# Two-layer hybrid backbone on one core: modulation computed by rows in pieces spread over the layer, no barrier between layers, and the DeltaNet preparation begun in the projection

## The chip, the core and the metric

One core of a Trainium2 chip runs the whole program. The metric is the device time of one execution in microseconds (us), median over runs. Engines are named as in the profile: PE is TensorE's matmul stream and PEld its weight load, DVE is VectorE, ACT ScalarE, POOL GpSimd, SP SyncE (here it only issues DMAs). A name with q, such as POOLq, is that engine's instruction queue. A difference of 0.2% (about 10 us) is what a measurement of this kernel can tell from no change.

## The reference

1024 latent tokens and 128 context tokens go through two layers. Each layer computes, for x of shape tokens x 1024:

```python
m = jnp.einsum('...d,de->...e', jax.nn.silu(cond), w_mod) + b_mod   # 3 x 1024 outputs
shift, scale, gate = split_cols(m, (D_MODEL, D_MODEL, D_MODEL))
h = rms_norm(x, norm_w) * (1.0 + scale) + shift
proj = jnp.einsum('btd,de->bte', h, lp['w_in'])                     # 9008 columns
# proj feeds three mixers: gated DeltaNet, grouped-query attention, Mamba-2 SSD
merged = sigmoid(g_a) * branch_a + sigmoid(g_b) * branch_b + sigmoid(g_c) * branch_c
x = x + gate * (merged @ w_out)
```

The conditioning vector does not depend on x, so shift, scale and gate of both layers can be computed at any time before they are used. A last RMSNorm ends the program. All data are fp32.

## The kernel before, in words

x is kept transposed, as 8 blocks (`KT`) of 128 channels by 1152 tokens (`T`; 9 tiles of 128, the last is the context). Every large product keeps fp32 precision by three matmuls (high times high, high times low, low times high) on operands split into two rounded parts: `h_hi`, `h_lo` for the activations, `w_hi`, `w_lo` for the weights. A **group** is 256 output columns: 144 matmuls of 384 columns, with its weights loaded into `w_raw` by SP and split by DVE (`split_group`). The projection is 36 groups.

A layer, inside a loop over the two layers, is a row of stages with barriers between them. At a barrier each engine drains and waits for the other four. The stages that matter here:

- **Stage 0, norm and modulation.** ACT squares x, DVE sums, PE sums over channels, POOL takes the power -1/2 (`r_tok`), DVE spreads it on diagonals (`r_diag`), PE turns them into rows (`row_bc`). PE multiplies the two conditioning vectors by `w_mod`, six loads of 2 MB with three buffers; ACT copies the two result rows, PE turns them into columns (`mod`). Then DVE, ACT and DVE make wide, `h_hi` and `h_lo` for each of the 8 blocks ("the h chain"), and DVE splits the first weights. Barrier 0.
- **Stage 1, projection.** PE bound. ACT and DVE take the results out, POOL stores them (`leave` to `proj_d`). Barrier 1.
- **Stage 2, DeltaNet preparation**, 9 tiles: PE transposes and multiplies, ACT squares, DVE sums, POOL takes a power, ACT scales, DVE writes `g_out`. SP stores `g_out` whole (`gdn_tile_d`); the diagonal 32x32 blocks of it are also stored by themselves, for one direction by SP and for the other by POOL (`blocks_out`, `adiag_d`). POOL fills `g_row`, `g_col` and clears buffers at the stage's start. Barrier 2.
- **Stage 3, attention preparation**, 9 tiles with the chain DVE, POOL, DVE, ACT, PE, ACT. Loads of `u_raw` from `adiag_d` begin it. Barrier 3.
- Attention, SSD, DeltaNet scan and the branches follow; the change leaves them as they are, up to the last product (`w_out`), whose `merge_out` on DVE writes the new x. Barrier 13 ends the layer.

After the loop, x is transposed back tile by tile, squared, scaled and stored.

Of the kernel before, what the change touches and what calls it, by code (L numbers as in the profile page):

```python
# [80 lines left out]
NPH = 14  # L81
# [41 lines left out]
def backbone_kernel(nc, A, O, table, rope_table):  # L123
    with ExitStack() as ctx:
# [19 lines left out]
        adiag_d = dram("adiag_d", [2, P, SOLVE * SOLVE])  # L144
        adiag_p_d = dram("adiag_p_d", [2, 16, SOLVE * SOLVE])
# [137 lines left out]
        gin = [place(a, f"gin{n}", [P, 12, P]) for n in range(2)]  # L283
        g_row = [place(a, f"g_row{n}", [P, 2, GH * P], F32R) for n in range(2)]
        g_col = [place(a, f"g_col{n}", [P, 2, P], F32R) for n in range(2)]
        own = place(a, "own", [P, GH])
# [68 lines left out]
        a = fresh([ACTV[2] - 12288, 0, ACTV[2]])  # L355
        mod_rows = place(a, "mod_rows", [P, 3 * D_MODEL])
        a = fresh(WT)
        w_mod = [place(a, f"w_mod{n}", [P, KT, 2 * GW]) for n in range(3)]

        a = fresh(EV)  # L360
        x_tok = [place(a, f"x_tok{n}", [P, D_MODEL]) for n in range(2)]
        f_gain = place(a, "f_gain", [P, D_MODEL])
        rows_wide = place(a, "rows_wide", [P, D_MODEL])
        rows_in = place(a, "rows_in", [P, P])
# [50 lines left out]
        mod_col = sem("mod_col")  # L415
# [87 lines left out]
        ain_in = [sem(f"ain_in{i}") for i in range(2)]  # L503
        state_in = [sem(f"state_in{i}") for i in range(2)]
# [5 lines left out]
        g_pstored = [sem(f"g_pstored{i}") for i in range(2)]  # L510
# [9 lines left out]
        mod_in = [sem(f"mod_in{i}") for i in range(3)]  # L520
        scan_in = [[sem(f"scan_in{d}{i}") for i in range(2)] for d in range(2)]

        def barrier(e, l, k):

            e.sem_inc(waits_held, 1)
            e.drain().then_inc(phase_done, 1)  # L526
            e.wait_ge(phase_done, l * 5 * NPH + 5 * (k + 2))
            e.sem_inc(waits_held, 1)
# [6 lines left out]
        def first_barrier(e):  # L535
            e.drain().then_inc(phase_done, 1)
            e.wait_ge(phase_done, 5)
# [59 lines left out]
        def blocks_out(e, t, d):  # L597

            for c in range(4):
                at = slice(c * SOLVE, (c + 1) * SOLVE)  # L600
                src = g_out[t % 2][at, 6 * d].rearrange("p (h t) -> p h t", t=P)[:, :, at]
                dst = adiag_d[d, c * 32 + t * 4:c * 32 + t * 4 + 4] if t < NS else adiag_p_d[d].rearrange("(h c) n -> c h n", c=4)[c]
                e.dma_start(dst.rearrange("h (j i) -> j h i", i=SOLVE), src).then_inc((g_pstored if d else g_stored)[t % 2], 16)

        def stored_count(l, t):


            return (l * (5 - t % 2) + t // 2) * 5 * 16

        def pool_stored(l, t):  # L610

            return (l * (5 - t % 2) + t // 2) * 4 * 16
# [84 lines left out]
        def _(sp):  # L697
            sp.dma_start(cst[:], table.rearrange("p (c n) -> p c n", n=P)).then_inc(cst_in, 16)
            sp.dma_start(rope[:], rope_table.rearrange("p (t a d) -> p t a d", t=NT, a=2)).then_inc(cst_in, 16)

# [4 lines left out]
            for t in range(NT):  # L705
                if t >= 2:
                    sp.wait_ge(tok_turned, t - 1)
                src = xsm[t * P:(t + 1) * P] if t < NS else A["x_prompt"].rearrange("b t d -> (b t) d")
                sp.dma_start(x_tok[t % 2][:], src).then_inc(tok_in[t % 2], 16)
            sp.drain().then_inc(phase_done, 1)  # L710

            with sp.Fori(0, DEPTH) as l:

                wm = A["w_mod"][l].rearrange("(k p) n -> p k n", p=P)
                for g in range(6):
                    if g >= 3:
                        sp.wait_ge(mod_used, l * 6 + g - 2)
                    sp.dma_start(w_mod[g % 3][:], wm[:, :, g * 2 * GW:(g + 1) * 2 * GW]).then_inc(mod_in[g % 3], 16)
                sp.wait_ge(mod_used, l * 6 + 4)
                arrive(sp, l, 0)  # L720

# [3 lines left out]
                for run, (kind, pairs, col, _) in enumerate(PROJ_RUNS):  # L725
# [8 lines left out]
                    base += 2 * pairs  # L734
                sp.wait_ge(row_made, l * 2 + 1)
# [6 lines left out]
                sp.dma_start(flat_rows[512:576], ssm_rows[0:64, 4].bitcast(F32)).then_inc(row_out, 16)  # L742
                sp.wait_ge(row_out, l * 80 + 80)
# [3 lines left out]
                def g_store(t):  # L747
                    sp.wait_ge(gp_kk, l * NT + t + 1)
                    blocks_out(sp, t, 0)
                    sp.wait_ge(gp_v, l * NT + t + 1)  # L750
                    sp.dma_start(gdn_tile_d[t], g_out[t % 2][:]).then_inc(g_stored[t % 2], 16)
# [13 lines left out]
                for p in range(2):  # L765
                    sp.wait_ge(g_stored[p], (l + 1) * (5 - p) * 5 * 16)
                    sp.wait_ge(g_pstored[p], (l + 1) * (5 - p) * 4 * 16)


                for d in range(2):  # L770
                    sp.dma_start(u_raw[:, d], adiag_d[d]).then_inc(beta_in, 16)
                    sp.dma_start(u_raw[32 * d:32 * d + 16, 2], adiag_p_d[d]).then_inc(beta_in, 16)

                with sp.Fori(0, 3) as i:
                    for p in range(2):
                        sp.wait_ge(transposed, nth(l, i * 2, 1, 5) + (p + 1))
                        ain_load(i * 2 + (p + 2), p)
                sp.wait_ge(transposed, nth(l, 7, 1, 5))
                ain_load(8, 0)
# [153 lines left out]
                barrier(sp, l, 13)  # L933
# [3 lines left out]
            for t in range(NT):  # L937
                sp.wait_ge(x_new, t + 1)
# [7 lines left out]
        def _(pe):  # L946
# [3 lines left out]
            pe.wait_ge(cst_in, 80)  # L950
            pe.transpose(bank(7, 24), rows_in[0:24], ident[0:24, 0:24]).then_inc(cond_t, 1)
            for t in range(NT):
                pe.wait_ge(tok_in[t % 2], 16 * (t // 2) + 16)
                if t >= 2:
                    pe.wait_ge(first_c, t - 1)
                for k in range(KT):
                    last = pe.transpose(bank(2 * (t % 2), P, k * P), x_tok[t % 2][:, k * P:(k + 1) * P], ident)
                last.then_inc(tok_turned, 1)
            first_barrier(pe)
# [8 lines left out]
            with pe.Fori(0, DEPTH) as l:  # L968


                def mod_columns(first, count, dst):

                    pe.wait_ge(mod_row, l * 6 + (first + count) // 4)
                    pe.sem_inc(waits_held, 1)
                    for b in range(count):
                        last = pe.transpose(bank(dst, 2, 32 + 2 * b), mod_rows[0:2, (first + b) * P:(first + b + 1) * P], ident[0:2, 0:2])
                    last.then_inc(mod_col, 1)
                for g in range(6):
                    pe.wait_ge(mod_in[g % 3], l * 32 + 16 * (g // 3) + 16)
                    if g >= 2:  # L980
                        pe.wait_ge(mod_row, l * 6 + g - 1)
                    for k in range(KT):
                        last = pe.matmul(bank(6 + g % 2)[0:2], cond[:, k:16:8], w_mod[g % 3][:, k],
                                         start=(k == 0), stop=(k == KT - 1))
                    last.then_inc(mod_used, 1)
                    if g == 1:
                        pe.wait_ge(n_add, l * (KT - 1) + KT - 1)
                        for t in range(NT):
                            last = pe.matmul(bank(2, 1, t), tmp[:, t * P:(t + 1) * P], ones[:, 0:1], start=True, stop=True)
                        last.then_inc(n_mm, 1)  # L990
# [1563 lines left out]
```

## Time and profile before

| | us |
|---|---|
| median of 3 runs | 4798.93 (4793.77 to 4803.2) |
| profiled execution, its time | 4772.26 |
| profiled execution, span of the core | 4770.5 |

Busy share of the span: PE 86%, DVE 45%, ACT 22%, POOL 13%. The profiled execution ran 0.56% below the median of the runs.

The page's table of slices cuts the span into 40 equal parts. A timeline row gives start, duration, engine and line, operation, output and inputs, and in brackets how long the engine sat idle before it and what released it.

### The profile page before, as it was taken

To read this page: it belongs to the slowest core of one execution; us is meant where nothing else is said; L and a number is where in the kernel's file an instruction comes from. 1 tells how busy PE (TensorE), PEld (TensorE's weight loads), DVE (VectorE), ACT (ScalarE), POOL (GpSimd) and SP (SyncE) were. 2 spreads that over 40 slices of the span, in tenths; PEclk is the share of its full clock that TensorE was granted. 3 is DMA by queue.
4 is the path that set the end of the run, shared out by engine and by line. 5 is a ranking of instruction groups with operands and counts; after the bars stand their busy time and mean duration, and the time that the engine had idled before them with its cause. 6 is when DMAs were issued, how large, how long until landed. Compare 5 with 4: busy or idle time off the path is not lost.

```text
span 4770.5 us, 64010 instructions
## 1 busy us (share of the span) xinstructions
PE 4117.2 (86%) x24849; PEld 3850.1 (81%) x24849; DVE 2153.1 (45%) x2548; ACT 1038.3 (22%) x1855; POOL 600.1 (13%) x725
## 2 busy tenths in 40 slices
PE   6999999974898968868879999999649989678698
PEld 2999999974887838868849999999648877478688
DVE  3432541116665782245345235311266667723563
ACT  2110111013444510220021012010233454102200
POOL 0010000025100150000000000000350002400000
PEclk7999999987998979989989999999859989789799
DMA  6222222225002442533252222222530034435332
GB/s 225 83 90 81 80 89 94 84 93 192 13 14 77 158 159 95 159 120 115 78 182 91 87 79 85 89 93 75 172 102 14 14 100 158 141 109 164 102 123 92
DMA packets 421562, 497.62 MB, mean 104 GB/s; under 512 B 77602, under 2 KB 357508, under 8 KB 413772
## 3 DMA queue, kind: packets, MB, share of 16 engines
q1 hardware_dynamic: 354840, 384.79, 24.5%
q0 software_dynamic: 33856, 94.70, 5.3%
q10 hardware_dynamic: 32636, 15.04, 1.1%
q8 instruction: 146, 2.39, 0.2%
q14 instruction: 84, 0.69, 0.0%
HBM read 325.08 MB, written 169.37 MB: 104 GB/s over the span
## 4 chain that ended last, share of the span: by engine, by line
PE 71%; DVE 7%; DMA 6%; issue 6%; SPq 3%; DVEq 3%; POOL 2%; ACT 1%; POOLq 1%; ACTq 1%
PE PSUM L680 15%; PE PSUM L682 14%; PE PSUM L681 14%; PE PSUM L1121 5%; PE PSUM L1268 4%; PE PSUM L1142 3%; PE PSUM L1110 2%; PE PSUM L1111 2%; SPq L899 2%; PE PSUM L1371 1%; PE PSUM L1372 1%; PE PSUM L1373 1%; DMA g_XY<-xy_d 1%; PE PSUM L1227 1%; DMA xin<-proj_d 1%
## 5 line engine op out<-in xcount | busy, mean ns | idle before, releaser
L680 PE MATMUL PSUM<-h_hi,w_hi 128*128 128x384 f32 x3456 | 1160.3, 336 | 38.2 <-DVEq L526 30.0
L681 PE MATMUL PSUM<-h_lo,w_hi 128*128 128x384 f32 x3456 | 1158.6, 335 | 0.0
L682 PE MATMUL PSUM<-h_hi,w_lo 128*128 128x384 f32 x3456 | 1158.2, 335 | 0.0
L680 PEld LDWEIGHTS PSUM<-h_hi,w_hi 128*128 128x128 f32 x3456 | 652.1, 189 | 39.3 <-issue 30.2
L681 PEld LDWEIGHTS PSUM<-h_lo,w_hi 128*128 128x128 f32 x3456 | 652.2, 189 | 0.0
L682 PEld LDWEIGHTS PSUM<-h_hi,w_lo 128*128 128x128 f32 x3456 | 651.9, 189 | 0.0
L664 DVE CAST w_hi<-w_raw 128x2048 fp32r<-128x2048 f32 (+1 forms) x104 | 118.9, 1143 | 722.6 <-PE PSUM L682 584.1
L1781 POOL DMA_DIRECT2D proj_d<-leave x140 | 80.9, 578 | 1684.6 <-ACT leave L1497 650.7
L680 PE MATMUL PSUM<-b_hi,w_hi 128*128 128x384 f32 x768 | 263.7, 343 | 27.9 <-DVE w_lo L666 10.8
L1121 PE MATMUL PSUM<-v_all,prob_t 128*128 128x64 f32 x2336 | 283.6, 276 | 2.3 <-DVE prob_t L2260 2.2
L1121 PEld LDWEIGHTS PSUM<-v_all,prob_t 128*128 128x128 f32 x2336 | 279.1, 196 | 4.6 <-issue 3.5
L681 PE MATMUL PSUM<-b_lo,w_hi 128*128 128x384 f32 x768 | 261.9, 341 | 0.0
L682 PE MATMUL PSUM<-b_hi,w_lo 128*128 128x384 f32 x768 | 261.6, 341 | 0.0
L2197 DVE TENSOR_REDUCE row_max<-PSUM 128x1 f32<-128x1152 f32 (+1 forms) x144 | 178.3, 1238 | 158.1 <-PE PSUM L1111 158.0
L666 DVE TENSOR_TENSOR w_lo<-w_raw,w_hi 128x2048 fp32r<-128x2048 f32 (+1 forms) x104 | 221.3, 2128 | 8.7 <-issue 0.9
L1497 ACT ACTIVATE leave<-PSUM 128x1152 f32<-128x1152 f32 x60 | 68.1, 1135 | 678.8 <-PE PSUM L682 678.8
L1142 PE MATMUL PSUM<-cst,prob 128*128 128x128 f32 x1168 | 162.2, 283 | 14.9 <-ACT prob L1602 9.7
L680 PEld LDWEIGHTS PSUM<-b_hi,w_hi 128*128 128x128 f32 x768 | 148.6, 194 | 31.7 <-issue 25.9
L1268 PE MATMUL PSUM<-g_XY,g_t 128*128 128x128 f32 x576 | 84.2, 308 | 102.3 <-DMA g_XY<-xy_d 93.8
L1110 PE MATMUL PSUM<-k_hi,q_now 128*128 128x512 f32 (+1 forms) x400 | 152.4, 381 | 16.7 <-ACT prob_t L1608 12.7
L1602 ACT ACTIVATE prob<-PSUM,row_max 128x1152 f32<-128x1152 f32 (+1 forms) x144 | 161.4, 1121 | 21.8 <-PE PSUM L1142 11.6
L1268 PEld LDWEIGHTS PSUM<-g_XY,g_t 128*128 128x128 f32 x576 | 78.7, 219 | 105.6 <-DMA g_XY<-xy_d 52.3
(310 smaller groups left out, 6588.2 us busy)
## 6 DMA issues: line engine op xcount, KB each, us to landing
w_raw<-in_w_in SPq DMA_DIRECT2D x70, 1024.0 KB, 4.8
proj_d<-leave POOLq DMA_DIRECT2D x140, 512.0 KB, 2.9
g_t<-gdn_tile_d SPq DMA_DIRECT2D x36, 1024.0 KB, 8.2
gdn_tile_d<-g_out SPq DMA_DIRECT2D x18, 1792.0 KB, 7.6
wide<-proj_d SPq DMA_DIRECT2D x48, 576.0 KB, 3.7
w_mod<-in_w_mod SPq DMA_DIRECT2D x12, 2048.0 KB, 16.9
xs<-ssm_tok_d SPq DMA_DIRECT2D x36, 640.0 KB, 4.7
ssm_tok_d<-x_rest SPq DMA_DIRECT2D x36, 512.0 KB, 3.2
```

The source lines that it names most:

```text
L664: dve.tensor_copy(w_hi[p][:, 0:kt], w_raw[p][:, 0:kt])
L666: dve.tensor_tensor(w_lo[p][:, 0:kt], w_raw[p][:, 0:kt], w_hi[p][:, 0:kt].bitcast(F32), ALU.subtract).then_inc(w_ready[p], 1)
L680: pe.matmul(dst, wh, x_hi[:, k, lo:hi], start=(k == 0), stop=False)
L681: pe.matmul(dst, wh, x_lo[:, k, lo:hi], start=False, stop=False)
L682: last = pe.matmul(dst, wl, x_hi[:, k, lo:hi], start=False, stop=(k == kt - 1))
L899: sp.dma_start(gd[d]["XY"][t % 2][at, :, at], src.rearrange("h x (j i) -> j h x i", i=SOLVE)).then_inc(scan_in[d][t % 2], 16)
L1110: pe.matmul(dst, q_now[u][:, h], k_hi[:, g, col:col + width], start=True, stop=False)
L1121: last = pe.matmul(bank(7, AD, h * AD), prob_t[s][:, j], v_all[:, kt, g * AD:(g + 1) * AD], start=(j == 0), stop=(j == len(key_tiles) - 1))
L1142: last = pe.transpose(dst, prob[s][:, j * P:(j + 1) * P], ident)
L1268: last = pe.matmul(bank(n, P, h * P), lhs(h), rhs(h), start=True, stop=True)
L1602: act.activation(prob[s][:, 0:width], PSUM[:, 1536 * s:1536 * s + width], ACT.Exp, bias=row_max[:, u, h:h + 1], accum_out=row_sum[:, u, h: ...
L2197: dve.tensor_reduce(row_max[:, u, h:h + 1], PSUM[:, 1536 * (h % 2):1536 * (h % 2) + nk * P], AX_X, ALU.max, negate=True).then_inc(at_m, 1)
```

## The change

- **Modulation by need.** Before the loop only the 2048 columns of shift and scale of layer 0 are multiplied (four loads of 2 MB, four buffers). The 1024 columns of the gate of each layer are multiplied in four products of 256 columns after the projection's runs 0 to 3 (`gate_products`). Shift and scale of layer 1 are multiplied in eight products of 256 columns in stage 3, one per tile (`next_columns`, `w_next`). The loop's body is the same for both layers, so layer 1 does the eight products too, and nothing uses them.
- **No barrier between layers.** Barriers 0 and 13 and the one ahead of the loop are gone. x is squared and summed block by block while `w_out` is multiplied (`add_square`). DVE splits the first weights ahead of the h chain. The small vectors of a layer are loaded by POOL (`vec_load`), at the end of the layer before, where ACT loaded them.
- **First group by blocks.** The first projection group goes over k in the outer loop, one step for each block that the h chain has made.
- **The start.** Input tiles have four buffers, where they had two.
- **DeltaNet preparation begun in the projection.** POOL fills `g_row`, `g_col` and loads the first rows, and SP loads the first two `gin` tiles, during the last projection run. POOL doesn't wait for its last stores ahead of barrier 1. Its other clearing is spread over tiles 3 to 5.
- **No block stores.** `blocks_out` is gone. In stage 3 SP reads the diagonal blocks from `gdn_tile_d` (`blocks_in`, 40 transfers a layer, five behind each of eight tiles).
- **The last norm** uses one sum for all tiles, where each tile had a square with its own sum and power.

```diff
-        def blocks_out(e, t, d):
-            for c in range(4):
-                ...
-                e.dma_start(dst.rearrange("h (j i) -> j h i", i=SOLVE), src).then_inc(...)
+        def blocks_in(e, c, d):
+            at = slice(c * SOLVE, (c + 1) * SOLVE)
+            for h in range(GH):
+                e.dma_start(u_raw[c * 32 + h:c * 32 + 32:GH, d].rearrange("t (j i) -> t j i", i=SOLVE),
+                            gdn_tile_d[0:NS, at, 6 * d, h * P + c * SOLVE:h * P + c * SOLVE + SOLVE]).then_inc(beta_in, 16)
+            e.dma_start(...)                                            # the context tile
...
+            def mod_product(dst, w):
+                for k in range(KT):
+                    last = pe.matmul(dst, cond[:, k:16:8], w[:, k], start=(k == 0), stop=(k == KT - 1))
+                last.then_inc(mod_used, 1)
...
+                def first_group():
+                    ...
+                    for k in range(KT):
+                        pe.wait_ge(h_made, l * KT + k + 1)
+                        for b in range(2):
+                            ...
+                            for c in range(3):
+                                ...  # three matmuls
...
+                def gate_products(run):
+                    if run < 4:
+                        if run:
+                            pe.wait_ge(mod_row, rows_done(l, run - 1))
+                        pe.wait_ge(mod_in[2], 16 + (l * 4 + run + 1) * 16)
+                        mod_product(bank(6, GW)[0:2], w_gate)
+                    ...
                 for run, (kind, pairs, col, _) in enumerate(PROJ_RUNS):
                     ...
+                    gate_products(run)
                     decay_products(run)
...
                 for t in range(NT):                                     # stage 3 on PE
                     if t + 2 < NT:
                         ain_turn(t + 2)
                     if t:
                         stack(t - 1)
+                    if t:
+                        next_columns(t - 1)
+                    if t < NS:
+                        pe.wait_ge(mod_in[t % 2], 16 + (l * 4 + t // 2 + 1) * 16)
+                        mod_product(bank(5, GW)[0:2], w_next[t % 2])
...
+                next_load(0)                                            # stage 3 on SP
+                next_load(1)
+                for t in range(2, 10):
+                    if t < NT:
+                        sp.wait_ge(transposed, nth(l, t - 1, 1, 5))
+                        ain_load(t, t % 2)
+                    if t >= 4:
+                        next_load(t - 2)
+                    blocks_in(sp, (t - 2) // 2, t % 2)
...
-                barrier(pe, l, 13)
+                norm_sums(l + 1)
```

On PE at the top of a layer, before, between the third product of the modulation and the projection (`w_mod`: the modulation's weights, 512 columns; L965: the norm's rows; L976: rows turned into columns):

```order
L965 MATMUL PSUM<-r_diag,cst 128x128 x8
L983 MATMUL PSUM<-w_mod_243,cond 2x512 x7
L976 MATMUL PSUM<-cst,mod_rows 128x2 x15
L983 MATMUL PSUM<-w_mod_244,cond 2x512 x7
L983 MATMUL PSUM<-w_mod_245,cond 2x512 [waits mod_row,mod_in2]
L983 MATMUL PSUM<-w_mod_245,cond 2x512 x7
L976 MATMUL PSUM<-cst,mod_rows 128x2 [waits mod_row]
L691 UNCONDITIONAL_BRANCH [waits phase_done]
L680 MATMUL PSUM<-h_hi,w_hi_84 128x384 [waits acc_free0]
```

The same place now; the `w_mod` rows stand ahead of the loop and run once:

```order
L1001 MATMUL PSUM<-w_mod_249,cond 2x512 [waits mod_row,mod_in3]
L1007 MATMUL PSUM<-cst,mod_rows 128x2 x15
L1033 MATMUL PSUM<-cst,vec_in 128x125 [waits n_ms]
L1024 MATMUL PSUM<-r_diag,cst 128x128 [waits n_diag,acc_free1]
L1042 ISA [waits acc_free0,w_ready0]
L1049 MATMUL PSUM<-h_hi,w_hi_84 128x384 [waits h_made]
```

The wait for all engines (`phase_done`) has become a wait for one block of h (`h_made`), and the products for the gate no longer stand ahead of the projection.

On POOL at the end of the projection, before (`leave`: the projection's results; `g_row`, `g_col`: operands of stage 2):

```order
L1782 DMA proj_d<-leave_95 128x128
L691 REGISTER_ALU [waits leave_out1]
L1793 MEMSET beta_p 128x96 [waits phase_done]
L1797 TENSOR_SCALAR g_row_162<-own 128x1024
L1797 TENSOR_SCALAR g_row_163<-own 128x1024
L1803 MEMSET w_inv 128x3072
L1813 DMA g_row_162<-cumrow_d 2x2x512
L1814 DMA g_col_164<-cumrow_d 8x2x128
```

And now, from the last run of the projection on:

```order
L1884 TENSOR_TENSOR own<-cst 128x4 [waits row_out]
L1853 TENSOR_SCALAR g_row_162<-own 128x1024
L1863 DMA g_row_162<-cumrow_d 2x2x512
L1853 TENSOR_SCALAR g_row_163<-own 128x1024
L1873 DMA proj_d<-leave_94 128x1024 [waits leave_ready0]
L1873 DMA proj_d<-leave_95 128x1024 [waits leave_ready1]
L1874 DMA proj_d<-leave_95 128x128
L1898 MEMSET beta_p 128x96 [waits phase_done]
```

The fill and the loads of `g_row` have moved ahead of the last stores and of the barrier (`phase_done`), and the wait for the last store (`leave_out1`) ahead of the barrier is gone.

On PE in stage 3, one tile, before (`ain`: the tile's input; `q_hl`, `k_hh`, `k_ll`: its split queries and keys):

```order
L1073 MATMUL PSUM<-cst,ain_228 128x128 [waits a_v,scaled]
L1083 MATMUL PSUM<-cst,q_hl_216 128x128 [waits a_q,a_split]
L1083 MATMUL PSUM<-cst,q_hl_216 128x128 x7
L1085 MATMUL PSUM<-cst,k_hh_234 128x128
L1086 MATMUL PSUM<-cst,k_ll_236 128x128
```

And now:

```order
L1143 MATMUL PSUM<-cst,ain_228 128x128 [waits a_v,scaled]
L1153 MATMUL PSUM<-cst,q_hl_216 128x128 x7
L1155 MATMUL PSUM<-cst,k_hh_235 128x128
L1156 MATMUL PSUM<-cst,k_ll_237 128x128
L1007 MATMUL PSUM<-cst,next_rows_254 128x2 [waits mod_row]
L1001 MATMUL PSUM<-w_next_251,cond 2x256 [waits mod_in0]
L1001 MATMUL PSUM<-w_next_251,cond 2x256 x7
```

Two small transposes, which wait for ACT's copy, and a product of eight matmuls, which waits for a load, now stand between one tile's transposes and the next tile's.

## Rows read from the trace of the kernel before

**Rows 1.** A stretch of projection: length, busy us (instructions) of PE, PEld, DVE, ACT, POOL.

```profile
core 0: us, PE busy (x) PEld busy (x) DVE busy (x) ACT busy (x) POOL busy (x), PEclk, DMA share, GB/s
150.00:200.00 50.00, 50.00 (x291) 50.00 (x290) 27.05 (x21) 9.71 (x16) 4.30 (x8) 1.00 0.25 90
```

**Rows 2.** The same view of four other stretches.

```profile
0.00:114.05 114.05, 71.52 (x230) 29.79 (x231) 41.24 (x62) 35.73 (x44) 7.25 (x17) 0.79 0.62 226
1026.15:1048.69 22.54, 0.00 (x0) 0.00 (x1) 0.00 (x0) 1.13 (x1) 14.60 (x16) 0.61 0.32 98
1048.69:1133.40 84.71, 46.10 (x288) 40.98 (x289) 46.04 (x81) 28.35 (x63) 37.06 (x59) 0.84 0.84 286
1133.40:1208.85 75.45, 37.84 (x166) 31.27 (x167) 58.47 (x73) 30.78 (x66) 41.45 (x29) 0.59 0.20 56
```

**Rows 3.** Timeline of PE, from the start to the first projection group.

```profile
33.81 15.86 PE L983 MATMUL PSUM<-w_mod,cond 128*2 128x512 f32 x32 [3.23 <-DMA w_mod<-in_w_mod]
...
82.69 1.12 PE L976 MATMUL PSUM<-cst,mod_rows 2*128 2x2 f32 x16 [0.77 <-ACT mod_rows L1434]
...
114.05 0.68 PE L680 MATMUL PSUM<-h_hi,w_hi 128*128 128x384 f32 x1 [15.02 <-DVEq L526]
...
119.87 0.34 PE L680 MATMUL PSUM<-h_hi,w_hi 128*128 128x384 f32 x1
```

**Rows 4.** Timeline of DVE, layer 0, the h chain and the first weight split.

```profile
84.38 3.19 DVE L1977 SCALAR_TENSOR_TENSOR wide<-x_sb,gain,row_bc 128x1024 f32<-128x1024 f32 x4
87.48 1.54 DVE L1988 SCALAR_TENSOR_TENSOR h_lo<-wide,mod,h_hi 128x1024 fp32r<-128x1024 f32 x2
...
111.09 2.29 DVE L666 TENSOR_TENSOR w_lo<-w_raw,w_hi 128x2048 fp32r<-128x2048 f32 x1
```

**Rows 5.** Timelines between the layers: DVE, PE, POOL and ACT.

```profile
2375.07 0.73 DVE L2401 SCALAR_TENSOR_TENSOR x_sb<-PSUM,half_gate,wide 128x256 f32<-128x256 f32 x2
...
2404.26 1.36 DVE L1956 TENSOR_TENSOR tmp<-tmp,wide 128x1152 f32<-128x1152 f32 x1 [0.16 <-issue]
...
2416.50 1.85 DVE L1948 TENSOR_SCALAR r_diag<-cst,r_tok 128x128 f32<-128x128 f32 x9
...
2436.61 3.18 DVE L1977 SCALAR_TENSOR_TENSOR wide<-x_sb,gain,row_bc 128x1024 f32<-128x1024 f32 x4
...
2405.67 2.17 PE L989 MATMUL PSUM<-cst,tmp 128*128 128x1 f32 x18 [1.03 <-DVE tmp L1956]
...
2427.12 7.03 PE L983 MATMUL PSUM<-w_mod,cond 128*2 128x512 f32 x16
...
2466.27 0.68 PE L680 MATMUL PSUM<-h_hi,w_hi 128*128 128x384 f32 x1 [15.01 <-DVEq L526]
...
2408.13 1.79 POOL L1765 TENSOR_TENSOR r_tok<-stat,minus_half 128x9 f32<-128x9 f32 x1 [263.06 <-DVE stat L1958]
...
2427.23 1.13 ACT L1440 ACTIVATE row_bc<-PSUM 128x1152 f32<-128x1152 f32 x1 [1.62 <-PE PSUM L965]
```

**Rows 6.** Chain that ended last, layer 0: start, us, what, at barriers 1 and 2.

```profile
1028.64 2.66 DMA proj_d<-leave
...
1031.62 2.36 POOLq L526
...
1124.85 8.28 POOLq L526
```

**Rows 7.** Stage 2, both layers: busy us, mean ns, idle before, releaser.

```profile
L2134 DVE TENSOR_TENSOR g_out<-PSUM,e_rest 128x512 f32<-128x512 f32 x36 | 23.2, 684 | 21.8 <-DMA adiag_d<-g_out 21.6
```

**Rows 8.** Timeline of DVE in stage 3, the same step of two tiles.

```profile
1177.28 0.82 DVE L2166 TENSOR_TENSOR qk<-qk_c,qk_s 128x640 f32<-128x640 f32 x1
...
1184.09 0.82 DVE L2166 TENSOR_TENSOR qk<-qk_c,qk_s 128x640 f32<-128x640 f32 x1
```

**Rows 9.** Chain that ended last, DeltaNet scan: back-to-back matmuls of 128 columns.

```profile
1923.61 13.48 PE PSUM L1268 x120
```

**Rows 10.** Timeline of DVE, the first tile of the output.

```profile
4746.35 1.28 DVE L2522 SCALAR_TENSOR_TENSOR x_tok<-PSUM,r_tok,f_gain 128x1024 f32<-128x1024 f32 x1 [0.66 <-POOL r_tok L1930]
```

**Rows 11.** DMA queue of ACT (loads of `gin` in runs of 512 bytes): packets, MB, share of 16 engines' span.

```profile
q10 hardware_dynamic: 32636, 15.04, 1.1%
```

More of the change, by code:

```diff
@@ L734, in _ @@
                     base += 2 * pairs
+                    if run < 4:
+                        gate_load(run)
                 sp.wait_ge(row_made, l * 2 + 1)
@@ L968, in _ @@
             with pe.Fori(0, DEPTH) as l:
[L971 to L981, printed above, removed]
-                    for k in range(KT):
[L983 to L990, printed above, removed]
-                        pe.wait_ge(vec_loaded, l * (22 * 16) + 22 * 16)
-                        pe.transpose(bank(0, NV), vec_in[0:NV], ident[0:NV, 0:NV]).then_inc(vec_t, 1)
-                    if g == 2:
-                        sums_to_rows(l * 2)
-                    if g == 3:
-                        mod_columns(0, 16, 1)
@@ new lines, in _ @@
+            act.drain()
+            for k in range(KT):
+                if k >= 3:
+                    act.wait_ge(n_add, k - 2)
+                act.activation(wide[k % 2][:] if k else tmp[:], x_sb[:, k], ACT.Square).then_inc(n_sq, 1)
+            for g in range(4):
+                act.wait_ge(mod_used, g + 1)
+                act.activation(mod_rows[0:2, g * 512:(g + 1) * 512], bank(4 + g % 2)[0:2], ACT.Copy).then_inc(mod_row, 1)
+            act.wait_ge(mod_used, 5)
+            act.activation(mod[:, 0:16], bank(7, 32).rearrange("p (k c) -> p k c", c=2), ACT.Copy).then_inc(cond_t, 1)
@@ L1821, in _ @@
+                barrier(pool, l, 1)
+                pool.memset(beta_p[:], 0.0)
+                pool.memset(u_raw[:, 2], 0.0)
+                pool.drain().then_inc(g_clear, 1)
+                pool.sem_inc(g_clear, 1)
                 for t in range(NT):
@@ L1940, in _, with norm_stat @@
             dve.drain()
-            dve.tensor_scalar(cond[:], cond[:], 0.5, None, ALU.mult)
-            first_barrier(dve)
+            dve.tensor_scalar(cond[:], cond[:], 0.5, None, ALU.mult).then_inc(cond_t, 1)
+            def norm_stat(i):
+                dve.wait_ge(n_mm, i + 1)
+                dve.tensor_scalar(stat[:, 0:NT], bank(6, NT), 1.0 / D_MODEL, EPS, ALU.mult, ALU.add).then_inc(n_ms, 1)
+            for k in range(1, KT):
+                dve.drain()
+                dve.wait_ge(n_sq, k + 1)
+                dve.tensor_tensor(tmp[:], tmp[:], wide[k % 2][:], ALU.add).then_inc(n_add, 1)
+            norm_stat(0)
             def diagonals(u):
@@ L2109, in _ @@
                     base += 2 * pairs
+                    if run == 4:
+                        dve.wait_ge(mod_used, gate_done(l, 4))
+                        modulation(16, 8, bank(7, 16).rearrange("p (k c) -> p k c", c=2))
+                        dve.drain()
+                        dve.tensor_scalar(half_gate[:], mod[:, 16:24], 0.5, None, ALU.mult)
                     decay_values(run)
```

404 lines of the change are left out of this document (227 added, 177 removed).

## The prediction

> **What bounds the kernel now.** I read the page first, then stretches, then the chain and the timelines around each edit. The projection is PE bound: in 50 us of it PE is busy for 50.00 at full clock, one matmul each 50/291 = 0.172 us, so a group of 144 takes 24.8 [rows 1]. Nothing that only relieves another engine helps there, and each PE instruction added there costs its full time. The change works elsewhere. Ahead of the projection the trace spends 114 us in which PE is busy for 71.5, on the modulation, and waits 15.0 at the end for DVE's drain [rows 2, 3]. Between the layers it takes from 2375.8 (the last write of x) to 2466.27 [rows 5]. After each projection PE has no work for 22.54, and in the two preparation stages (84.7 and 75.5 us) it is busy half the time [rows 2]: these are chains through several engines.
>
> **Overlap of the first group.** Before, the h chain starts at 84.38, the split ends at 113.4 (111.09 + 2.29), PE starts at 114.05 [rows 3, 4]. PE then runs 18 matmuls in 5.82 us, half speed; at full speed these are 3.1, so the group ends at 114.05 + 24.8 + 2.7 = 141.6. From chain start to group end: 57.2. Now PE starts when block 0 is made: two blocks of wide (3.19) and one h_lo (1.54) after the chain's start, 4.7. A block then comes each 3.1 us (3.19/2 + 1.54), and PE needs 18 x 0.172 = 3.1 for it. PE has idled ahead of it, so I keep the 2.7 of half speed: 4.7 + 24.8 + 2.7 = 32.2. DVE's second split (3.6) is ready before PE asks for it. Gain 25 in each layer, **50**. Bounds: 28 a layer if PE stays at full clock, 7 if it runs all 144 at half clock.
>
> **The h chain starts earlier, layer 0.** PE carries the start: two products in 15.86, two more at 7.03, the norm's sums 2.17, columns 0.77 + 1.12 [rows 3, 5], 34 us in all. They begin when x has been turned and the first load is there. Before, PE was through with x at 30.6 and waited to 33.81. DMA moves 226 GB/s at a share of 0.62, about 365 when full; x, constants and the first 2 MB are 7.3 MB, so 22 us with the start; 30.6 is the other bound. I take 25, nearer to the transfers since four buffers keep them going. Columns at 59, vectors, norm rows (18 x 0.112 = 2.0 [rows 9]) and the split of 3.6 on DVE bring the chain's start to 65, from 84.38: **19**, between 14 and 23. All four loads are 13.6 MB, 39 us, and the fourth is asked for at 50, so they are covered by 11 us.
>
> **The same, between layers.** After the last write of x: square 1.13 (as ACT's pass over the same shape), add 1.36, sums 2.17, power 1.79, diagonals 1.85, rows 2.0, out 1.13 [rows 5, 9]; 11.4, with eight hand-overs of 0.1 and 3 for PE at half clock 15.5. The split (3.6 with vector copies) fits beside the last two. So the chain starts at 2391.3, not 2436.61: **45**, between 42 and 48. All weights are long loaded, and POOL's 22 small loads lie beside the products of w_out.
>
> **Gate products, in the projection.** A product of 512 columns takes 7.03 for 16 records, 0.44 each [rows 5]; 128 columns take 13.48/120 = 0.112 [rows 9]. 256 columns lie between; time follows columns, so 0.22, 3.5 a product. Four and eight transposes of 0.07: 14.7 a layer on PE, uncovered: **-29**. Bounds 8 to 29 a layer. SP blocks on each gate load until PE is through with the one before; the weights queued behind are then a group late, and have another group (25 us) in hand.
>
> **Barrier 1.** PE ends at 1026.15 and starts at 1048.69. The barrier opens at 1034.0, after POOL's store has landed (1031.3) and its drain (2.36) [rows 6]; the 14.7 behind it are POOL filling rows and loading them, now hidden in the last run of 100 us. The wait for the store is gone, but I let the drain take as long. **29** for both. Bounds: 11 a layer if the drain takes the 8.28 of barrier 2 from the store's issue, 19 if nothing.
>
> **Stage 2.** DVE waited 21.6 us for block stores, both layers [rows 7]; they are gone. Stores and loads still keep DMA busy (0.84 of the stretch [rows 2]), so of 10.8 a layer I take 8: **16**, between 0 and 22.
>
> **Barrier 2.** POOL's drain of 8.28 behind its stores [rows 6] goes. Next is late: SP waits for the last tile's store, then puts two loads of 1 MB ahead of the input of tile 2, 5.7 us at 365 GB/s. Of 8.3 I keep 4: **8** for both, between 2 and 17.
>
> **Stage 3.** DVE sets 6.81 a tile [rows 8]. PE is busy 37.84 of 75.45 at a granted clock of 0.59 [rows 2], 4.2 a tile, about 3 at full clock. With 3.5 for the product and the small transposes it has 6.7 a tile at full clock: just covered. The loop through PE, ACT and DVE stretches by some 0.3, the tail by 2: 4 a layer, **-8**, twice because layer 1 does it for nothing. If the cover fails it is the first rival.
>
> **The end.** Square, add, sums and power now stand ahead of the first output tile (about 7 us with hand-overs); before it came at 4746.35 [rows 10], 5 us after x. The tiles behind lose their square and power. **0**, within 4.
>
> **Sum.** 50 + 19 + 45 - 29 + 29 + 16 + 8 - 8 = 130 us (2.7%). The profiled execution took 4772.26, so a like one takes about 4642. The median of runs lies 26.7 above it; I forecast the median: 4799 - 130 = 4669.
>
> **Rivals.**
> - *PE stays at half clock in stage 3.* 4.4 + 7.2 = 11.6 a tile against 6.81, eight tiles: 38 a layer in place of 4, +68: 4737. For: clock 0.59 there now. Against: the long products of rows 3 ran at nearly full speed once they were under way, and PE would have no idle time. 0.10.
> - *The block loads hold up stage 3.* Each tile has five transfers of together 1152 runs of 128 bytes. ACT's queue spent 1.1% of 16 x 4770 us on 32636 packets, 26 ns each [rows 11]. Over all engines that is 1.9 us a tile and hidden; if four of the five go over eight engines and one over four, the busiest has 4 x 32 + 32 = 160, 4.1 us, with the 1 MB (2.9) and the input (1.2) 8.2 a tile, 1.4 above DVE: +14 with stage 3's 8 replaced, 4683. The Trainium skill's DMA: Bandwidth & Descriptors (Why a DMA increments its semaphore by 16 and not by 1) says that a DMA is spread over the largest number up to 16 that divides both sides' slowest dimension. These have 8 tiles or 4 heads there, so by that rule this case would hold, 4683; no row here shows it. 0.08.
> - *PE runs the first group at half clock*, fed block by block: 18 a layer lost, 4705. Against: it needs all the time that it has. 0.05.
> - *More than counted*: stage 3 covers its products wholly and barrier 2 gives its 8.3: 4652 or less. 0.10.
> - *Slower.* The narrow products let the granted clock fall in the projection. If a whole group after each of the eight gate products ran at half clock, 8 x 24.8 = 198 us: 4867. It decides from 130 us, 16 behind each product. Against it, [rows 3]: two narrow products take 15.86 where 14.06 would be full speed, so the clock rises in them. 0.03.
>
> **Chances.** Forecast 0.64, the others as given: 0.10, 0.08, 0.05, 0.10, 0.03. The range reaches from 4632 (every gain at its upper half) to 4712, taking in the third rival and leaving out the first and last, 0.13, and some extremes. 0.2% is about what a measurement of this kernel can tell from no change: faster 0.96, same 0.01, slower 0.03.
>
> **What would show it.** First projection matmul near 70, group 1 from near 97; between layers less than 22 us from the last write of x to PE's next matmul of the projection; gate products 3.5 each; PE starting stage 2 some 8 us after the projection, no DVE wait for a store in its tiles; stage 3 below 7.3 a tile at a clock above 0.9. The prediction is wrong if stage 3 takes over 90 us, or if the h chain starts after 75 because the loads of w_mod come late.

## The result and the profile after

The changed kernel takes 4736.04 us (median of 4 runs, 4731.09 to 4745.39), the kernel before 4800.78 (4793.77 to 4803.20): ratio 0.987, 95% interval 0.9851 to 0.9889. A second measurement, beside 9 runs of before, gave 0.9908 (0.9885 to 0.9932). The change makes the kernel faster by 0.9 to 1.3%, 65 us in the first measurement, half of the forecast 130, and 4736 lies outside the range of 4632 to 4712. One execution of the kernel of experiment 5 took 6816.67 us at a granted clock of 0.565, where its others took 4700.77 to 4723.82, and it is left out of that ratio. The profiled execution of after took 4745.39, that of before 4772.26, 28.5 below its median, so the two traces differ by only 26.9. The difference must therefore be made up stretch by stretch.

In the text below, "after" is the changed kernel and "before" the kernel before it. The windows of after, layer 0 from the start to the end of stage 3, then the products of branches a and b (below "the branches"), those of `w_out`, and the way to layer 1's first group. Columns as in [rows 1].

```profile
0.00:84.49 84.49, 50.86 (x190) 23.98 (x190) 21.04 (x32) 26.21 (x29) 18.71 (x39) 0.84 0.86 267
84.49:1011.89 927.40, 922.91 (x5291) 911.66 (x5291) 305.15 (x264) 125.23 (x170) 86.14 (x147) 0.99 0.25 88
1011.89:1017.70 5.81, 0.00 (x1) 0.01 (x1) 0.00 (x0) 1.13 (x1) 1.17 (x3) 0.93 0.26 102
1017.70:1090.03 72.33, 46.79 (x289) 42.02 (x289) 45.51 (x81) 28.34 (x63) 21.92 (x28) 0.85 0.81 293
1090.03:1183.95 93.92, 62.33 (x311) 35.23 (x311) 58.19 (x74) 31.99 (x74) 41.45 (x29) 0.81 0.51 154
2166.67:2296.25 129.58, 108.77 (x577) 107.18 (x577) 66.54 (x53) 10.82 (x10) 11.66 (x22) 0.91 0.43 109
2296.25:2400.00 103.75, 101.95 (x576) 101.62 (x576) 41.11 (x43) 10.52 (x9) 0.00 (x0) 0.98 0.29 97
2400.00:2422.16 22.16, 8.63 (x38) 8.00 (x38) 12.48 (x24) 5.17 (x6) 7.11 (x9) 0.64 0.48 186
```

The first, third, fourth and fifth row answer to [rows 2]. The sixth answers to a stretch that the prediction did not look at, the branches. The same view of before, layers 0 and 1:

```profile
2151.72:2271.49 119.77, 106.32 (x576) 104.49 (x576) 66.49 (x53) 10.77 (x10) 0.00 (x0) 0.94 0.34 114
4519.66:4637.36 117.70, 105.81 (x577) 104.52 (x577) 66.52 (x53) 10.78 (x10) 0.00 (x0) 0.94 0.35 116
```

POOL did nothing there before; now it issues 22 DMAs (11.66 us, x22), and PE, with the same work, needs 9.8 us more, in layer 1 11.9. Of the 9.8, PE idles 7.4 more (20.8 against 13.5) and is busy 2.4 longer, at a granted clock of 0.91 where it was 0.94. The DMA view of after from 2171 to 2193 us has the late weight load (KB, us from issue to landing; before's two such loads have a median of 4.8), and PE's timeline the wait:

```profile
w_raw<-in_w_branch_a SPq DMA_DIRECT2D x1, 512.0 KB, 12.8
...
2201.05 0.69 PE L697 MATMUL PSUM<-b_hi,w_hi 128*128 128x384 f32 x1 [7.37 <-DVEq L2485]
```

Stretch by stretch, in us saved (before less after, by PE's starts, both layers together where there are two):

| stretch | forecast | measured |
|---|---|---|
| start to the first projection group (h chain 19, overlap 25) | 44 | 29.6 |
| projection (gate products) | -29 | -31.2 |
| end of projection to stage 2 (barrier 1) | 29 | 33.5 |
| stage 2 and barrier 2 (16 and 8) | 24 | 23.9 |
| stage 3 | -8 | -36.5 |
| branches up to w_out | 0 | -21.7 |
| w_out of layer 0 to layer 1's first group (45 and 25) | 70 | 68.9 |
| w_out of layer 1 to the end | 0 | 0.5 |
| sum | 130 | 67.0 |

The sum, 67.0, lies near the 65 of the medians. What the two traces differ by elsewhere, 40 us against after, lies in stages whose code the change leaves as it was. Part of it comes and goes: the SSM preparation of layer 0 took 152.7 in after, 141.4 in its second profile. Attention took 313.4 and 327.2 in the two layers of before, and 323 to 327 in both layers of all later profiles but one (317.8). There is one profile of before only, so whether the 313.4 of layer 0 was chance is not shown; that the medians agree with the sum speaks for it. Three rows of the table miss, by 14.4, 28.5 and 21.7.

**The start.** PE's timeline of after, to be read against [rows 3]:

```profile
17.87 1.97 PE L988 MATMUL PSUM<-cst,x_in 128*128 128x128 f32 x8 [3.77 <-DMA x_in<-in_x_sample]
30.55 4.41 PE L988 MATMUL PSUM<-cst,x_in 128*128 128x128 f32 x24 [10.72 <-DMA x_in<-in_x_sample]
...
39.53 15.59 PE L1001 MATMUL PSUM<-w_mod,cond 128*2 128x512 f32 x32 [3.17 <-DMA w_mod<-in_w_mod]
...
84.49 0.69 PE L1049 MATMUL PSUM<-h_hi,w_hi 128*128 128x384 f32 x1 [7.66 <-DVE h_lo L2077]
```

From the first product to the first matmul of the group it is 45.0 (forecast 44.7); but the products begin at 39.53, not 25, since a tile of x keeps PE waiting for 10.72.

**Stage 3.** The chain that ended last, one tile of after:

```profile
1132.33 1.40 PE PSUM L1153 x8
1133.73 0.21 PE PSUM L1155
...
1134.58 0.30 PE PSUM L1007 x2
1134.88 4.28 PE PSUM L1001 x16
1139.16 0.82 PE PSUM L1143 x6
...
1140.76 1.03 ACT q_stack L1633
1141.79 0.28 ACT k_hi L1634
1142.07 0.29 ACT k_lo L1635
1142.35 0.14 issue
1142.49 1.32 PE PSUM L1153 x8
```

A tile takes 10.16 us (1132.33 to 1142.49) and DVE, which set 6.81 before [rows 8], is not in it. It is a loop of PE and ACT: stacking (the transposes of the tile's split queries and keys), columns, the product of 4.28, the turn of the next tile (the transposes of its input), then ACT's square and copies, for which PE waits 2.5 us.

Two things make the tile longer than 6.81, and the granted clock is one of them. From the tile that begins at 1122.17 on, PE's stacking and the start of the product run at half clock (transposes 0.21 us apart, the product 4.26 to 4.58 long). The tile ahead of that one ran at full clock (transposes 0.11 apart, the product 3.62):

```profile
1113.55 1.09 PE L1153 MATMUL PSUM<-cst,q_hl 128*128 128x128 f32 x8 [1.33 <-DVE k_ll L2264]
...
1115.22 3.62 PE L1001 MATMUL PSUM<-w_next,cond 128*2 128x256 f32 x16
...
1122.17 1.48 PE L1153 MATMUL PSUM<-cst,q_hl 128*128 128x128 f32 x8 [2.52 <-ACT k_lo L1635]
```

That is 8.62 us from stacking to stacking. So at full clock the loop itself is 1.8 longer than DVE's 6.81, and the half clock adds the other 1.5 of the 3.35.

### The profile page after: what moved, and what is told of

The parts are those of the page before. It is cut to its first block, busy times and chain, and to the rows that moved or that the text cites. A ratio compares the mean times of both kernels' runs of the same rounds, so it can differ in the third digit from the quotient of the medians.

```text
span 4743.7 us, 64363 instructions
## 1 busy us (share of the span) xinstructions
PE 4160.5 (88%) x25139; PEld 3882.2 (82%) x25139; DVE 2171.4 (46%) x2549; ACT 1039.4 (22%) x1862; POOL 586.7 (12%) x711
## 4 chain that ended last, share of the span: by engine, by line
PE 70%; issue 11%; DMA 6%; DVE 5%; SPq 3%; DVEq 2%; POOL 1%; ACT 1%; POOLq 0%; ACTq 0%
PE PSUM L697 14%; PE PSUM L699 14%; PE PSUM L698 14%; PE PSUM L1202 5%; PE PSUM L1349 4%; PE PSUM L1223 3%; PE PSUM L1001 2%; PE PSUM L1191 2%; PE PSUM L1192 2%; SPq L931 2%; DMA g_XY<-xy_d 1%; DMA xin<-proj_d 1%; PE PSUM L1255 1%; PE PSUM L1254 1%; PE PSUM L1308 1%
## 5 line engine op out<-in xcount | busy, mean ns | idle before, releaser
L697 PE MATMUL PSUM<-h_hi,w_hi 128*128 128x384 f32 x3360 | 1126.8, 335 | 9.0 <-DVEq L2175 9.0
L698 PE MATMUL PSUM<-h_lo,w_hi 128*128 128x384 f32 x3360 | 1124.7, 335 | 0.0
L699 PE MATMUL PSUM<-h_hi,w_lo 128*128 128x384 f32 x3360 | 1124.6, 335 | 0.0
L697 PEld LDWEIGHTS PSUM<-h_hi,w_hi 128*128 128x128 f32 x3360 | 632.4, 188 | 13.5 <-DVEq L2175 9.6
L698 PEld LDWEIGHTS PSUM<-h_lo,w_hi 128*128 128x128 f32 x3360 | 632.4, 188 | 0.0
L699 PEld LDWEIGHTS PSUM<-h_hi,w_lo 128*128 128x128 f32 x3360 | 632.3, 188 | 0.0
L2174 DVE SCALAR_TENSOR_TENSOR leave<-leave,PSUM 128x1152 f32<-128x1152 f32 x32 | 43.3, 1353 | 275.3 <-ACT leave L1558 275.0
```

What stands on the lines that cost most here:

```text
L697: pe.matmul(dst, wh, x_hi[:, k, lo:hi], start=(k == 0), stop=False)
L698: pe.matmul(dst, wh, x_lo[:, k, lo:hi], start=False, stop=False)
L699: last = pe.matmul(dst, wl, x_hi[:, k, lo:hi], start=False, stop=(k == kt - 1))
```

## Experiments

There are twelve kernels: eleven edit the changed kernel, and one is the changed kernel again. They ran on three chips whose time of before was 4802.85, 4785.28 and 4793.93, so the ratios to before on the same chip are compared. The two ratios for after are 0.987 and 0.9908. Where the interval of a ratio overlaps theirs, the verdict rests on the stages in the profile.

**1. The small loads on another queue.** `vec_load` issues its 22 loads on ACT: first thing in the program, and behind the copies of `b_hi` in the branches.

```diff
+            vec_load(0)
             act.wait_ge(cond_t, 1)
...
                 arrive(act, l, 12)
+                vec_load(NEXT)
...
-                        pool.dma_start(qk_gain[:, at + h], A[name][l].partition_broadcast(P)).then_inc(vec_loaded, 16)
+                        act.dma_start(qk_gain[:, at + h], A[name][l].partition_broadcast(P)).then_inc(vec_loaded, 16)
```

> The changed kernel with the 22 small loads of the modulation (norm weights, biases, rows, gains) issued on ACT's queue in place of POOL's, at the start and in the branches; nothing else. Theory: on POOL's queue these loads hold up the other transfers. In the trace of after, 704 packets of 0.44 MB take 45.1% of 16 engines x 34 us, 0.35 us each, while the trace of before has 26 ns a packet for its 32636 on ACT's queue. Then the first product of the start begins near 28 us, not 39.5, the weights of the second branch group land in about 5 us, not 10 to 13, and each layer's branches take 119 us, not 129.6: 12 + 20 = about 30 us less, 4706. Rival: it is the small loads themselves, or the volume of x and w_mod, and the queue does not matter: 4736 within 5. Second rival: the issues, 0.5 us each, delay ACT's first copies by 7 us or more and the start gains nothing: 4716.

Measured 0.9859 (0.9826 to 0.9891): as after. First product at 41.04, branches and w_out together 236.5 and 235.6 us, where after has 235.9 and 235.7. The queue's own share is small, and yet little else moves. DMA view of this run, 2158 to 2180 us in 40 slices (busy tenths of the 16 engines, then GB/s), and the queue of ACT:

```profile
DMA  0010111110000000000001397430000000000005
GB/s 19 19 39 13 12 17 25 25 37 21 21 20 22 18 22 8 21 20 20 17 24 68 155 358 266 179 127 19 22 18 22 22 20 22 21 17 10 22 20 183
...
q10 hardware_dynamic: 2258, 0.42, 8.4%
```

Apart from one burst of 4 us, DMA moves about 20 GB/s. My theory, that POOL's queue was to blame, fell. The first rival held. The second held too at the start: ACT was issuing until 20.2 us, and PE waited 11.08 for its first copies.

**2. Fewer of them.** Each gain vector is spread over the partitions once, in place of 8 and 2 times.

```diff
-                    for h in range(heads):
-                        pool.dma_start(qk_gain[:, at + h], A[name][l].partition_broadcast(P)).then_inc(vec_loaded, 16)
+                    pool.dma_start(qk_gain[:, at], A[name][l].partition_broadcast(P)).then_inc(vec_loaded, 16)
...
+                dve.tensor_scalar(qk_gain[:, 1:AH], qk_gain[:, 0:1].broadcast_to([P, AH - 1, AD]), AD ** -0.5, None, ALU.mult)
+                dve.tensor_copy(qk_gain[:, 9:10], qk_gain[:, 8:9])
...
```

> The changed kernel with 14 small loads in place of 22 at each of the three places: each gain vector of 64 is spread over the partitions once, not once a head (8 and 2 times), and DVE copies it to the heads (three operations, 0.5 us). Theory: the spreading loads themselves (128 packets of 256 bytes each from one place) hold up what is queued beside them, on any queue: in the run with the loads on ACT's queue DMA moved about 20 GB/s from 2158 to 2178 us with the engines' share near 0.1, and the weight load asked for at 2170.3 took 14 us. Eight of the 22 gone, which are more than half of the packets: the first product begins near 32 us, not 39.5, the branches take about 124, not 129.6: 7 + 2 x 6 = 19 us less, 4717. Rival: the other 14 do it, or the number of packets is not what holds: 4736 within 5.

Measured 0.9813 (0.9765 to 0.9860), profiled span 4678.5. PE's timeline of it:

```profile
17.29 5.69 PE L988 MATMUL PSUM<-cst,x_in 128*128 128x128 f32 x32 [1.82 <-DMA x_in<-in_x_sample]
26.30 13.89 PE L1001 MATMUL PSUM<-w_mod,cond 128*2 128x512 f32 x32 [3.32 <-DMA w_mod<-in_w_mod]
...
68.59 0.69 PE L1049 MATMUL PSUM<-h_hi,w_hi 128*128 128x384 f32 x1 [8.38 <-DVE h_lo L2079]
```

First product at 26.3 (the prediction had 25, this run's theory 32), first group at 68.6 (the prediction near 70), branches and w_out 225.6 and 224.9, 10 and 11 us less. So eight of the 22 loads hold nearly the whole loss, 16 + 10 + 11 = 37 us by the profile, twice the 19 that I expected from their share of the packets.

**3. The same loads later.** POOL waits for the second load of `w_mod`, and between the layers for `m_in`.

```diff
-            vec_load(0)
...
+            pool.wait_ge(mod_in[1], 16)
+            vec_load(0)
...
+                pool.wait_ge(m_in, l * KT + 1)
+                pool.sem_inc(waits_held, 1)
                 vec_load(NEXT)
```

> The changed kernel with the 22 small loads asked for later: at the start behind the landing of the second load of w_mod, between the layers beside the products of w_out (POOL waits for the first merged block). Theory: only their place costs. Then the first product begins near 28 us and the chain of h about 11 earlier, the branches take 119: 11 + 20 = 31 us less, 4705. Rival: the cost moves with them, to the later loads of w_mod and to the weights of w_out, whose groups then wait: within 10 of 4736.

Measured 0.9876 (0.9840 to 0.9912), no gain that the interval tells. The profile splits it: at the start the first group begins at 70.7 (13.8 earlier); in the branches only 3.5 us a layer come back. The wait opened at 2207 us, still in the branches (2136.76 to 2262.12) and not beside w_out as I had written, so the loads met other weight loads. The cost moves with them there.

**4. Same number, other addresses.**

```diff
-                        pool.dma_start(qk_gain[:, at + h], A[name][l].partition_broadcast(P)).then_inc(vec_loaded, 16)
+                        pool.dma_start(qk_gain[:, at + h], A["w_in"][l][0:P, (at + h) * AD:(at + h + 1) * AD]).then_inc(vec_loaded, 16)
```

> The changed kernel with each of its ten gain loads reading 128 different rows of w_in (256 bytes of each) in place of 128 times the same 256 bytes; number, size and queue of the packets stay. The gains are then not the reference's. Theory (the one place that is read 1280 times is what holds): first product near 27 us as in few_loads (26.3), the branches 226: 33 us less than after. Rival (small packets as such, on any address): as after, first product near 39.5, branches 236, time within 5.

Measured 0.9796 (0.9775 to 0.9817), 46 us below after on the same chip. The first product starts at 25.90, branches and w_out take 226.3 and 225.2: as with fewer loads. Against the second profile of after, the first group starts 12 us earlier and the two branches are 9 and 10 shorter, 31 of the 46; where the rest lies these profiles do not show. DMA views, 12 to 24 us (packets, MB, share of 16 engines); first after, then this run:

```profile
q0 software_dynamic: 191, 0.19, 70.0%
q1 hardware_dynamic: 262, 0.96, 21.8%
```

```profile
q1 hardware_dynamic: 1546, 4.31, 92.9%
q0 software_dynamic: 322, 0.32, 8.2%
```

In after 191 small packets take 0.70 x 16 x 12 / 191 = 0.70 us each and let 0.96 MB of x pass; with 128 different rows 322 packets take 0.049 each, and 4.31 MB pass. So it is neither the queue nor the number of packets, but the ten loads that read two places of 256 bytes, one eight times and one twice, 128 reads each time. Experiment 2, which keeps one such load of each place, loses almost nothing, so it takes the repetition and not one spread load.

**5. The product shortened.**

```diff
-                        mod_product(bank(5, GW)[0:2], w_next[t % 2])
+                        pe.matmul(bank(5, GW)[0:2], cond[:, 0:16:8], w_next[t % 2][:, 0], start=True, stop=True).then_inc(mod_used, 1)
```

> The changed kernel with each of the eight products of the next layer's shift and scale in stage 3 cut to its first matmul of 8 (1 record in place of 8 of each weight pair); the loads, copies, transposes and waits stay. It leaves out 7/8 of the sum, so layer 1's shift and scale are wrong. Theory: the stretch of stage 3 to 10.16 us a tile is a loop through PE and ACT (product 4.4, turn of the tile 0.9, ACT's square and copies 2.4, stacking 2.1, columns 0.4), in which the product counts fully. Then a tile falls to DVE's 6.8 and the stage from 94 to about 79: 30 us less in both layers, 4706. Rival: the loads (8 of 1 MB and 40 small block loads) hold the tiles: the stage stays over 90 and the time within 6 of 4736.

Measured 0.9819 (0.9771 to 0.9867). Stage 3 took 82.5 and 81.1, a tile 6.95:

```profile
1131.65 1.94 PE L1153 MATMUL PSUM<-cst,q_hl 128*128 128x128 f32 x8 [2.52 <-ACT k_lo L1635]
...
1138.60 1.94 PE L1153 MATMUL PSUM<-cst,q_hl 128*128 128x128 f32 x8 [2.52 <-ACT k_lo L1635]
```

All loads were still there, so they do not hold the tiles. PE still waits for ACT and not for DVE, and its stacking is at half clock throughout (1.94 for eight transposes, 1.09 at full): the loop without the product happens to be about as long as DVE's beat.

**6. The product at another place in PE's tile.** ACT copies the row ahead of its square.

```diff
                     if t:
-                        stack(t - 1)
-                    if t:
                         next_columns(t - 1)
                     if t < NS:
                         mod_product(bank(5, GW)[0:2], w_next[t % 2])
+                    if t:
+                        stack(t - 1)
```

> The changed kernel with PE's order in a tile of stage 3 changed: turn, columns, product, then stacking, in place of turn, stacking, columns, product; ACT copies the product's row ahead of the square. All work stays. Theory of the loop: the product then runs beside ACT's 2.4 us of square and copies, a tile takes about 7.8 in place of 10.16, the stage about 80 in place of 94: 28 us less in both layers, 4708. Rival (PE needs the time anyway, or the loads hold the tiles): the stage stays above 90, 4736 within 5.

Measured 0.9833 (0.9799 to 0.9866); stage 3 80.6 and 82.4. PE's timeline of this run:

```profile
1130.81 0.87 PE L1143 MATMUL PSUM<-cst,ain 128*128 128x128 f32 x6 [0.73 <-DVE qk L2246]
...
1131.83 3.62 PE L1001 MATMUL PSUM<-w_next,cond 128*2 128x256 f32 x16
...
1137.63 0.87 PE L1143 MATMUL PSUM<-cst,ain 128*128 128x128 f32 x6 [0.73 <-DVE qk L2246]
```

6.82 a tile, not the 7.8 that I expected: PE again waits for DVE, and the product, 3.62 at full clock, costs the tile nothing. Two things changed at once: the product now lies beside ACT's copies, and the stacking no longer falls to half clock (1.09 in every tile shown). The loop of 8.62 at full clock shows that the order is needed for it.

**7. Tile 2's input ahead.**

```diff
+                sp.wait_ge(transposed, nth(l, 1, 1, 5))
+                ain_load(2, 0)
                 for p in range(2):
                     sp.wait_ge(g_stored[p], (l + 1) * (5 - p) * 16)
...
-                    if t < NT:
+                    if 2 < t < NT:
```

> The changed kernel with the input of tile 2 of stage 3 asked for ahead of the two loads of 1 MB and of the wait for the last store; the products stay where they are. Theory: of the stage's 93.9 us, 18 longer than before, 4 to 6 are this input (the combined run's 77 against 81 of product_first) and 12 the loop: the stage takes 88 to 90, 10 us less in both layers. Rival: the loop hides the input, as PE has to do the products anyway: 93 to 94, time within 4 of after.

Measured 0.9877 (0.9851 to 0.9902) beside 0.9908 for after on the same chip. PE's wait for the input of tile 2, in after and in this run:

```profile
1105.20 1.51 PE L1143 MATMUL PSUM<-cst,ain 128*128 128x128 f32 x6 [12.36 <-DMA ain<-proj_d]
...
1097.58 1.54 PE L1145 MATMUL PSUM<-cst,ain 128*128 128x128 f32 x6 [7.68 <-DVE qk L2248]
```

Stage 3 took 89.7 and 88.4: 4 and 5 us less, so the rival, that the loop hides it, falls. The two intervals overlap, so this rests on the stage.

**8. The overlap undone.**

```diff
                     pe.wait_ge(acc_free[0], l * NG + 1)
+                    pe.wait_ge(h_made, l * KT + KT)
                     for k in range(KT):
-                        pe.wait_ge(h_made, l * KT + k + 1)
```

> The changed kernel with PE waiting for all eight blocks of h ahead of the first group, whose order stays block by block. Theory of the prediction: the overlap is worth nearly a group's making, seven blocks of 3.1 = 22 us a layer: 44 us more, 4780. Rival: PE is at half clock or fed slowly in the overlapped group, so that less is lost: under 25 us more, below 4761.

Measured 0.9983 (0.9961 to 1.0005): 36 to 54 us lost against the two ratios of after. By the profile the group starts 18.6 later after the first product, and 19.8 later behind the layer, and PE waits 27.97 ahead of it where after has 7.66:

```profile
103.69 0.69 PE L1049 MATMUL PSUM<-h_hi,w_hi 128*128 128x384 f32 x1 [27.97 <-DVE h_lo L2077]
```

The overlap is real, near the expected 22 a layer.

**9 to 12. Together, and the changed kernel again.**

> The loads on ACT's queue and the product first, and in stage 3 the input of tile 2 is asked for ahead of the two loads of 1 MB and of the wait for the last store. Theory: 30 + 28, and 6 a layer for tile 2's input (12.4 us waited in the trace of after, 5.4 before): 70 us less than after, 4666. Rival: the parts share their gain, or the clock takes it back in the stages behind: 4700.

> 14 loads, late, with the product first and tile 2's input ahead in stage 3. Theory: 31 (start and branches) + 19 (product first) + 14 (tile 2's input, as the combined run's stage of 77 against 81 shows, in both layers) less what both share: 4680. Rival: the loads' cost moves with them: 4700.

> The changed kernel as it is, beside the three others of this call on one chip. 0.987 of before, and in a second profile of it the stages ahead of and in stage 3 within 1 us of the first profile, while the SSM preparation of layer 0 (152.7 us in the first profile, 137 to 144 in all others) comes out near 140.

> 14 loads at their old place, product first, tile 2's input ahead. Theory: 14 (start) + 20 (branches) + 34 (stage 3, 77 for 94 twice) = 68 us less than after, 0.973 of before. Rival: the late loads of the run best, 0.975, were as good: within 3 us of it.

`combined` (loads on ACT, product first, tile 2's input ahead) measured 0.9798 (0.9767 to 0.9829), less than expected by the loads, which had gained nothing; 4703 is the number of its rival, but not for the rival's reason. Its stage 3 took 76.9 and 77.0. `best` (14 loads, late, with both changes of stage 3) 0.975 (0.9713 to 0.9786), 4669 for an expected 4680. `after_again` 0.9908, its stages up to attention within 1.2 us of the first profile. `best2` (14 loads at their old place, product first, input ahead) 0.9716 (0.9699 to 0.9732): 4659.53 us, 86 below after on the same chip (expected 68) and the fastest kernel here. The intervals of `best` and `best2` overlap, so whether the old place of the 14 loads is the better one is not shown. Its stage 3, both layers:

```profile
1077.00:1153.80 76.80, 57.37 (x310) 33.25 (x310) 57.74 (x74) 33.17 (x74) 41.44 (x29) 0.86 0.63 189
3369.70:3446.70 77.00, 57.09 (x310) 33.16 (x310) 57.85 (x74) 33.39 (x74) 41.43 (x29) 0.83 0.63 188
```

77 us with all eight products in it, where before had 75.45 without them [rows 2].

## Why the prediction was half right

The forecast of 4669 missed the measured 4736 by 67 us, and three of its steps failed: the arrival of the input at the start (14 us of the table), the small loads beside the branches (22), and the cover of the products in stage 3 (28). Both signs that the prediction named for being wrong came: stage 3 took 93.9, over 90, and the h chain of layer 0 started at 79.79, behind 75, though a tile of x (10.72 us of waiting) was late more than `w_mod` (3.17). The rest was right in sum.

- **Overlap of the first group, h chain between the layers, gate products, barrier 1**: right in mechanism and size. The group ends 31.6 us after the chain's start (forecast 32.2; 79.79 to 111.36), the way between the layers is 22.3 long (forecast below 22), a gate product takes 3.62 (3.5), and PE starts stage 2 5.8 after the projection (8). The clock in the projection stays at 0.99 granted, so the rival for slower did not come. Nor did the first group at half clock: only its first 4 us ran so (matmuls 0.32 us apart until 88.47, 0.17 from then on).
- **Stage 2 and barrier 2**: the sum of 24 is right, the split is not. Stage 2's own work, to DVE's last output, went from 74.2 to 71.5 only; DVE's wait for the block stores is gone, but PE now waits 5.32 for a tile of `gin` and 1.22 for `g_col`: loads are late in place of the stores. Barrier 2 gave its 9.7 whole, and what I had put against it, tile 2's input behind 2 MB of `w_next`, fell into stage 3: 12.36 us of waiting where before had 5.40, worth 4 to 5 (experiment 7).
- **The h chain, layer 0**: forecast 19, measured 4.6 (84.38 to 79.79). The step that failed is "22 us with the start": I divided the bytes by the rate of a full DMA and left out the 22 small loads, because their bytes are few (0.44 MB). They hold the other loads back for some 15 us: between 12 and 24 us the queue of x moves 0.96 MB, and 4.31 when the ten loads read different rows (experiments 2 and 4).
- **"POOL's 22 small loads lie beside the products of w_out"** failed twice. In POOL's order they stand right behind barrier 10, at the head of the branches (2167.07), and there they are not free: the weight load of a group lands late and PE waits. They cost 21.7 us, with a forecast of 0; with eight loads fewer, 21 came back.
- **Stage 3**: forecast -8, measured -36.5. The step was "6.7 a tile at full clock: just covered". I compared PE's busy time with DVE's beat, but the product stands in PE's order between the stacking and the next tile's turn, and ACT's copies for the next stacking wait behind that turn. Cover asks for an idle gap at that place of the order, not for idle time in sum: PE was idle for 2.5 us a tile even at 10.16. At full clock, which the step assumed, this loop takes 8.62; the half clock on the stacking and the product's start makes it 10.16. Experiments 5 and 6 give 6.95 and 6.82 a tile. Of the stage's 18 us a layer, the late input of tile 2 is the 4 to 5 above.
- **The rivals**: half clock in stage 3 would have given 4737, by chance the time that came. It came in part: about half of a tile's excess over 6.81 is half clock, but the granted clock was 0.81 and the tile 10.16, not 11.6, and the rest of the loss lay elsewhere. The block loads over few engines (8.2 a tile) did not show: with every load in place experiments 5 and 6 ran at 6.95 and 6.82. By how many engines the rule of the Trainium skill's DMA: Bandwidth & Descriptors, cited there, spread them, no view here tells.

## What to carry to other kernels

Work put on an engine that idles half the time is free only where the idle time stands in its order; put it right ahead of the instruction that already waits, and draw the loop through all engines before adding up busy times. Count small loads by what they read, not by their bytes: a vector that several heads need should be spread over the partitions by one load and copied to the heads on the chip (37 us here for eight loads fewer). Ahead of "these loads lie beside X", find their place in the queue's order and what lands late there.

## What the runs showed of the hardware

Ten loads that spread two places of 256 bytes over 128 partitions, one eight times and one twice, slowed the transfers beside them (x, `w_mod`, `proj_d`, branch weights) while they ran. In the run on ACT's queue DMA moved about 20 GB/s while the engines' busy share was near 0.1, a state that looks idle in the page, and a load of 512 KB asked for at 2170.3 took 14.2 us; in before such loads took 4.8. With 128 different rows of the same size x and `w_mod` moved 4.31 MB in 12 us, where after moved 0.96. With one spread load of each place the first product started at 26.30, with none at 25.90; the five spread loads of 32 to 128 bytes a partition stay in every run. Whether the limit sits in the memory or on the way to it, no run here tells.
